# A transformer layer on one core: PE works on a constant tile before x arrives, x transposes through four banks, and the products with w_ck1 and w_cv1 go side by side

## The chip, the cores and the metric

The kernel runs on one core of a Trainium2 chip. The metric is the device time of one execution in microseconds (us). Three runs of the kernel before gave 1227.9, 1228.57 and 1229.16 us, with a median of 1228.57 us.

## The reference, cut to what matters

One layer of a decoder, everything in float32, for 256 tokens of width 1024:

```
h = rmsnorm(x, g_mix); z = h @ w_in              # 1024 -> 5184 columns
o_a = nsa_mixer(...)   # compressed, selected and windowed attention; 8 heads of 64
o_b = dsa_mixer(...)   # an indexer picks 64 keys per query; 8 heads of 64
merged = sigmoid(ga) * (o_a @ w_branch_a) + sigmoid(gb) * (o_b @ w_branch_b)
x = x + merged @ w_out
x = x + moe_ffn(rmsnorm(x, g_ffn), ...)          # top 4 of 32 experts, w_e1 1024x2048, w_e2 1024x1024
x = x + sigmoid(rmsnorm(x, g_ple) @ w_ple_gate) * (p @ w_ple)
```

Within `nsa_mixer` the compressed branch makes one key and one value from 32 tokens each, 15 of them in each of 2 groups:

```
def compress(z, pe, w1, w2):
    zb = z[:, cmp_tok] + pe[None, None, :, None, :]
    hdn = jax.nn.silu(jnp.einsum('bclgd,lde->bcge', zb, w1))    # w1: 32 x 64 x 64
    return jnp.einsum('bcge,ed->bcgd', hdn, w2)
k_cmp = rmsnorm(compress(k_cmp_raw, pe_ck, w_ck1, w_ck2), g_k)
v_cmp = compress(v_cmp_raw, pe_cv, w_cv1, w_cv2)
```

## The kernel before, in words

Each engine has its own program, written out by hand, and the engines meet in semaphores. TensorE (PE) follows the list `ORDER` at first. `T:G` transposes the gains g_mix, g_ple and g_ffn into gT. `T:X0` to `T:X3` transpose x, each two of its eight blocks of 128 columns, by four transposes of 128x128. `Z0` to `Z6` are the products with column chunks of w_in; the late chunks of w_in (the branch gates) are spread over the attention that follows. The letters `IX`, `DQ`, `DK`, `NQ`, `K`, `R` and `PE` after a `T:` are transposes of what the Z stages gave.

A job of the `T:` kind gets its PSUM bank by its place in the list `TJOBS`: `tbank(n)` returns bank 4 or 5 in turn and waits until the job two before it is evacuated (semaphore t_ev). The transposes stand at L1455. ScalarE (ACT) evacuates all of them, those of x at L891, with the gain as scale, into hT. Z0 (L1507) starts on the first pair of blocks of hT once it is evacuated, and each further pair has its own wait. Z0 has 296 columns; the chunks after it have 512. The weight chunks go through four buffers, wbuf, and SyncE (SP) issues their loads at L712: chunk 0 right behind x, chunk 1 when the second half of x has landed, and the later ones when their buffer is free.

PE's program begins with a wait on ld_const: four small loads that ACT issues at L874 to L877 (the identity, g_mix, g_ple, g_ffn). VectorE (DVE) begins with a wait for both halves of x and with the sums of squares of x (L1092), from which GpSimd (POOL) makes the root of the mean (L807, L812, semaphore x_rs). ACT needs it when it evacuates Z0 (L952). POOL's first work is a memset of the tile `half`, 128x64 times -0.5 (L795), and its chain semaphore pool_ch counts it.

The attention runs over 24 units. In step u PE issues the scores of unit u (L1554), the transposes of unit u-3 (L1562), some passes of the late chunks of w_in (L1590) and the products with the values of unit u-4 (L1577, L1581), two heads at a time with their results in partitions 0 to 63 and 64 to 127. In step 1 comes the stage `HID` (L1535), the products of the compressed branch: for keys and then for values, 16 products with a stationary tile of 128x64 and a moving tile of 128x30, both results in partitions 0 to 63 of bank 7. ACT takes its exponential (L929), DVE finishes the silu (L1269 to L1274), and in step 5 the stage `CMPKV` multiplies with w_ck2 and w_cv2 (L1541, L1543).

After the attention come the two branch products (L1623), w_out (L1644), the router, and 32 experts. The weights of an expert, 12 MB, go through a ring of ten slots of 2 MB. SP issues the first five of these loads when the last output of the attention is evacuated (o_ev, L354 in `load`), the rest when later stages of PE free the space. PE multiplies with w_e1 at L432 and with w_e2 at L461. The last stage multiplies with w_ple_gate (L1712).

In the change, `glu` of the experts counts two steps with one semaphore in place of two, so that there are semaphores for the new ones.

Of the kernel before, what the change touches and what calls it, by code (L numbers as in the profile page):

```python
# [18 lines left out]
ALU = mybir.AluOpType  # L19
# [3 lines left out]
P = 128  # L23
SEQ, DM = 256, 1024
TT = SEQ // P
# [63 lines left out]

TJOBS = [x for x in ORDER if x.startswith("T:")]  # L90
for _u in range(STEPS):
# [23 lines left out]
def block_kernel(nc, io, out):  # L115
    ctx = ExitStack()
    with ctx:
# [37 lines left out]
        def bm(ap, n):  # L155
# [55 lines left out]
        ckr = work_small(4)  # L211
        ck2w = work_small(2, DH, parts=DH)

# [60 lines left out]
            sem(n) for n in ("ld_wab", "ld_bias", "st_er", "st_rep", "ld_route", "ld_b1", "ld_be2", "ld_p", "ld_ple", "ld_ple_gate"))  # L274
        piece = [sem(f"piece{i}") for i in range(NS)]
        ld_wo = [sem(f"ld_wo{n}") for n in range(2)]
        gates_ready, zeroed, x_sq, x_rs, t_ps, t_ev, z_ps, z_ev = (
# [9 lines left out]
            sem(n) for n in ("s_ps", "s_log", "s_exp", "s_prob", "bd_ready", "o_ps", "o_ev"))  # L287
        pr_ps, pr_used, mg_ready, wo_ps, x2_ready, f_sq, f_rs = (
            sem(n) for n in ("pr_ps", "pr_used", "mg_ready", "wo_ps", "x2_ready", "f_sq", "f_rs"))
        rt_ps, lg_ready, rt_exp, m_ready, rk_ps, wr_ready, wt_ready, hp_ready, b1_sub, b1_cast, ranks_taken, x2_taken, xr_ready, dup_ready, h0_ready, oe_zero = (  # L290
# [19 lines left out]
        def expert_sems(tag):  # L310
            names = ("pieces_used", "s_ready", "sel_ready", "xe_ps", "xe_ready", "gc_ready", "lin_ready", "glu_ready", "sig_ready",
                     "act_ready", "at_ps", "at_ready", "wst_ps", "ws_ready", "wst_ready", "out_ready")
            return {n: sem(f"{n}_{tag}") for n in names}
# [306 lines left out]
        def expert_dve(ve, a):  # L620
# [20 lines left out]
            def glu(it, used):  # L641
                ve.wait_ge(s["pieces_used"], used)
                d.tensor_scalar(gc, ps[0][:, :], LIMIT, None, ALU.min).then_inc(s["gc_ready"], 1)  # L643
                d.tensor_scalar(lin, ps[1][:, :], LIMIT, -LIMIT, ALU.min, ALU.max).then_inc(s["lin_ready"], 1)
                ve.wait_ge(s["gc_ready"], it + 1)
                ve.wait_ge(s["lin_ready"], it + 1)
                d.scalar_tensor_tensor(lin, lin, 1.0, gc, ALU.add, ALU.mult).then_inc(s["glu_ready"], 1)
                ve.wait_ge(s["glu_ready"], it + 1)
                ve.wait_ge(s["sig_ready"], it + 1)
                d.tensor_tensor(act, lin, sg, ALU.mult).then_inc(s["act_ready"], 1)  # L650
# [45 lines left out]
        with nc.Block() as block:  # L696
            @block.sync
            def _(sp):
# [4 lines left out]
                for c, (o, n) in enumerate(CHUNKS):  # L703
# [9 lines left out]
                    if c == 1:  # L713
                        sp.dma_start(tab[0:BUCKETS, :], io["rel_bias"]).then_inc(ld_tab, 16)
                        sp.dma_start(tab[BUCKETS:BUCKETS + 1, :], io["negrow"]).then_inc(ld_tab, 16)
                        sp.dma_start(onehot, io["onehot"]).then_inc(ld_tab, 16)
                        sp.dma_start(const_all[:, P:545], io["consts"][:, P:545]).then_inc(ld_consts, 16)
                        for i, n in enumerate(("g_q_nsa", "g_k_nsa", "g_q_dsa", "g_k_dsa")):
                            sp.dma_start(gqk[:, i, :], io[n].to_broadcast([P, DH])).then_inc(ld_small, 16)
                        for i, n in enumerate(("pe_ck", "pe_cv")):  # L720
                            sp.dma_start(pe_in[:, i, :], io[n][0].rearrange("(l q) d -> l (q d)", q=2)).then_inc(ld_small, 16)
                        for i, n in enumerate(("w_ck2", "w_cv2")):
                            sp.dma_start(ck2w[:, i, :], io[n][0]).then_inc(ld_small, 16)
                        sp.dma_start(wr.rearrange("p (q r) n -> p q r n", r=RUN), io["w_router"][0].rearrange("(q p r) n -> p q r n", p=P, r=RUN)).then_inc(ld_route, 16)
                        sp.dma_start(br, io["b_router"].to_broadcast([P, NE])).then_inc(ld_route, 16)
# [145 lines left out]
            def _(sc):  # L871
# [6 lines left out]
                def tjob(name):  # L878
# [6 lines left out]
                    if kind == "G":  # L885
                        a.copy(gT, b[:, 0:24]).then_inc(t_ev, 1)
                        sc.wait_ge(t_ev, n + 1)
                    elif kind == "X":
                        for i in range(2):
                            k = 2 * t + i  # L890
                            l = a.activation(hTv[:, k, :], b[:, i * SEQ:(i + 1) * SEQ], ACT.Copy, scale=gT[:, k:k + 1])  # L891
                        l.then_inc(t_ev, 1)
                    elif kind == "IX":
# [30 lines left out]
                def stage_act(stage):  # L924
                    if stage.startswith("T:"):
                        tjob(stage)
                    elif stage == "HID":
                        sc.wait_ge(h_ps, 1)
                        a.activation(hsg, ps[7][0:DH, 0:60].rearrange("p (a n) -> p a n", a=2), ACT.Exp, scale=-1.0).then_inc(h_exp, 1)  # L929
# [156 lines left out]
            def _(ve):  # L1086
                d = nc.vector
                ch = Chain(ve, dve_ch)
                ve.wait_ge(ld_x, 16)
                ve.wait_ge(ld_xb, 16)  # L1090
# [137 lines left out]
                for u in range(NU + 2):  # L1228
# [37 lines left out]
                    if u == HIDDEN_AT:  # L1266
# [3 lines left out]
                        ch(d.reciprocal(hsg, hsg))  # L1270
                        ch(d.tensor_tensor(hid, hsg, ps[7][0:DH, 0:60].rearrange("p (a n) -> p a n", a=2), ALU.mult))
                        ve.wait_ge(zeroed, 1)
                        for g in range(2):
                            l = d.tensor_copy(hid4[:, g, :, 0:NCMP], bm(hid[:, 1, g * NCMP:(g + 1) * NCMP], 4))  # L1274
                        l.then_inc(hid_ready, 1)
# [157 lines left out]
            def _(te):  # L1433
                mm, tr = nc.tensor.matmul, nc.tensor.transpose
                te.wait_ge(ld_const, 16 * 4)

# [5 lines left out]
                def tjob(name):  # L1442
# [4 lines left out]
                    if kind == "G":  # L1447
                        tr(b[:, 0:16], grow, ident[0:16, 0:16])
                        for r in range(RUN):
                            l = tr(b[:, 16 + r:24:RUN], gffn[:, r:RUN * P:RUN], ident[0:KT // RUN, 0:KT // RUN])  # L1450
                    elif kind == "X":
                        te.wait_ge(ld_x if t < 2 else ld_xb, 16)
                        for i in range(2):
                            for q in range(TT):
                                l = tr(b[:, i * SEQ + q * P:i * SEQ + (q + 1) * P], x[:, q, (2 * t + i) * P:(2 * t + i + 1) * P], ident)  # L1455
                    elif kind == "IX":
# [34 lines left out]
                    l.then_inc(t_ps, 1)  # L1491

                for stage in ORDER:
                    if stage.startswith("T:"):
                        tjob(stage)
                    elif stage[0] == "Z":
# [29 lines left out]
                def stage_pe(stage):  # L1526
                    if stage.startswith("T:"):
                        tjob(stage)
                    elif stage == "HID":
                        te.wait_ge(ld_ck, 32)  # L1530
                        te.wait_ge(zb_ready, 1)
                        te.wait_ge(i_rl, 6)
                        for kv in range(2):
                            for l2 in range(16):
                                l = mm(ps[7][0:DH, kv * 30:(kv + 1) * 30], wck1[:, kv, l2, :], zb[:, kv, l2, :], start=l2 == 0, stop=l2 == 15)  # L1535
                        l.then_inc(h_ps, 1)
                    elif stage == "CMPKV":
                        te.wait_ge(hid_ready, 1)
                        te.wait_ge(o_ev, 1)
                        for g in range(2):  # L1540
                            mm(ps[6][0:NCMP, g * DH:(g + 1) * DH], hid[:, 0, g * NCMP:(g + 1) * NCMP], ck2w[:, 0, :], start=True, stop=True)  # L1541
# [224 lines left out]
```

## Time and profile before

| | |
|---|---|
| median of three runs | 1228.57 us |
| the profiled execution | 1228.02 us |
| its span, first to last instruction | 1226.1 us |
| PE busy | 1152.8 us, 94% |
| DVE, ACT, POOL busy | 271.0, 193.1, 35.8 us |
| read from HBM | 446.71 MB |
| mean over the span | 368 GB/s |

The span lies 1.9 us below the profiled execution's own time, which is 0.55 us below the median. A float32 product appears in the trace as two passes, each with a weight load (LDWEIGHTS, engine PEld) and a MATMUL (PE); a transpose has one pass. A MATMUL's duration is its latency: passes are pipelined, and the distance from start to start says what one costs.

### The profile page before, as it was taken

To read this page: it belongs to the slowest core of one execution; us is meant where nothing else is said; L and a number is where in the kernel's file an instruction comes from. 1 tells how busy PE (TensorE), PEld (TensorE's weight loads), DVE (VectorE), ACT (ScalarE), POOL (GpSimd) and SP (SyncE) were. 2 spreads that over 40 slices of the span, in tenths; PEclk is the share of its full clock that TensorE was granted. 3 is DMA by queue.
4 is the path that set the end of the run, shared out by engine and by line. 5 is a ranking of instruction groups with operands and counts; after the bars stand their busy time and mean duration, and the time that the engine had idled before them with its cause. 6 is when DMAs were issued, how large, how long until landed. Compare 5 with 4: busy or idle time off the path is not lost.

```text
span 1226.1 us, 15102 instructions
## 1 busy us (share of the span) xinstructions
PE 1152.8 (94%) x6374; PEld 490.5 (40%) x6374; DVE 271.0 (22%) x780; ACT 193.1 (16%) x411; POOL 35.8 (3%) x49
## 2 busy tenths in 40 slices
PE   7999999999999999998989889999989898988998
PEld 4455545453333343333333333333333343333344
DVE  1474543253111121111111111111112121111121
ACT  2223445131111111111111100000000010000011
POOL 2122100000000000000000000000000000000000
PEclk9999999999999999999999989999999999999999
DMA  8934070978999999999999999999999999999980
GB/s 281 333 138 172 35 206 32 416 247 346 394 432 437 429 427 431 431 435 429 431 432 435 424 430 429 433 431 430 430 433 433 432 430 433 433 431 430 425 360 35
DMA packets 39884, 448.41 MB, mean 366 GB/s; under 512 B 7407, under 2 KB 10576, under 8 KB 26306
## 3 DMA queue, kind: packets, MB, share of 16 engines
q1 hardware_dynamic: 38254, 441.66, 86.4%
q0 software_dynamic: 1264, 5.27, 1.2%
q10 hardware_dynamic: 324, 0.86, 0.3%
q8 instruction: 33, 0.54, 0.2%
q14 instruction: 9, 0.07, 0.0%
HBM read 446.71 MB, written 4.22 MB: 368 GB/s over the span
## 4 chain that ended last, share of the span: by engine, by line
PE 66%; DMA 31%; ACT 1%; issue 1%; DVE 0%; ACTq 0%
PE ps L432 21%; DMA wbuf<-in_w_e 15%; PE ps L461 12%; DMA ring<-in_w_e 12%; PE ps L1507 7%; PE ps L1590 5%; DMA wbuf<-in_w_ple_gate 3%; PE ps L404 3%; PE ps L395 3%; PE ps L1712 2%; PE ps L1623 2%; PE ps L1644 2%; PE ps L1554 2%; ACT xres L580 1%; PE ps L451 1%
## 5 line engine op out<-in xcount | busy, mean ns | idle before, releaser
L432 PE MATMUL ps<-ring,xres 128*64 128x512 f32 x1216 | 277.2, 611 | 18.1 <-DMA ring<-in_w_e 17.9
L432 PE MATMUL ps<-wbuf,xres 128*64 128x512 f32 x832 | 186.4, 602 | 11.2 <-DMA wbuf<-in_w_e 11.2
L643 DVE TENSOR_SCALAR oT<-ps 128x512 f32<-128x512 f32 x32 | 22.1, 692 | 706.1 <-PE ps L432 706.1
L432 PEld LDWEIGHTS ps<-ring,xres 128*64 128x64 f32 x1216 | 88.9, 141 | 195.2 <-issue 165.7
L461 PE MATMUL ps<-ring,xres 128*64 128x512 f32 x608 | 134.8, 595 | 12.5 <-ACT xres L580 12.5
L432 PEld LDWEIGHTS ps<-wbuf,xres 128*64 128x64 f32 x832 | 60.3, 138 | 129.7 <-issue 109.5
L461 PE MATMUL ps<-wbuf,xres 128*64 128x512 f32 x384 | 85.0, 595 | 8.1 <-ACT xres L580 8.1
L576 ACT ACTIVATE oT<-oT 128x512 f32<-128x512 f32 x30 | 18.9, 630 | 453.6 <-DVE oT L643 453.6
L1507 PE MATMUL ps<-wbuf,hT 128*128 128x512 f32 (+2 forms) x224 | 85.7, 540 | 0.0
L461 PEld LDWEIGHTS ps<-ring,xres 128*64 128x64 f32 x608 | 42.2, 137 | 91.8 <-issue 80.4
L404 PE MATMUL ps<-xres 64*128 64x512 f32 x256 | 63.6, 615 | 0.7 <-ACT xres L606 0.7
L1590 PE MATMUL ps<-wbuf,hT 128*128 128x512 f32 x128 | 59.8, 594 | 0.0
L1507 PEld LDWEIGHTS ps<-wbuf,hT 128*128 128x128 f32 x224 | 41.9, 190 | 38.8 <-issue 35.6
L395 PE MATMUL ps<-misc,gat 128*128 128x64 bf16 x1536 | 56.2, 197 | 0.5 <-DVE gat L1344 0.5
L395 PEld LDWEIGHTS ps<-misc,gat 128*128 128x128 bf16 x1536 | 56.0, 117 | 1.3 <-DVE misc L1379 1.3
L582 ACT COPY xres<-ps 128x512 f32<-128x512 f32 x30 | 17.6, 586 | 216.0 <-PE ps L461 216.0
L461 PEld LDWEIGHTS ps<-wbuf,xres 128*64 128x64 f32 x384 | 26.4, 137 | 58.4 <-issue 48.0
L404 PEld LDWEIGHTS ps<-xres 64*128 64x128 f32 x256 | 22.0, 186 | 41.8 <-issue 40.2
L618 DVE TENSOR_TENSOR xres<-ps,misc 128x512 f32<-128x512 f32 x32 | 22.1, 692 | 33.3 <-PE ps L395 33.3
L1712 PE MATMUL ps<-wbuf,ring 128*128 128x512 f32 (+1 forms) x80 | 27.9, 508 | 1.5 <-DMA wbuf<-in_w_ple_gate 1.5
L1590 PEld LDWEIGHTS ps<-wbuf,hT 128*128 128x128 f32 x128 | 22.3, 190 | 17.5 <-issue 17.4
L1644 PE MATMUL ps<-wbuf,hT 128*128 128x512 f32 x64 | 28.5, 594 | 0.0
(250 smaller groups left out, 788.7 us busy)
## 6 DMA issues: line engine op xcount, KB each, us to landing
ring<-in_w_e SPq DMA_DIRECT2D x51, 4096.0 KB, 37.2
wbuf<-in_w_e SPq DMA_DIRECT2D x36, 4096.0 KB, 37.3
ring<-in_w_e SPq DMA_DIRECT2D x14, 2048.0 KB, 28.6
wbuf<-in_w_in SPq DMA_DIRECT2D x9, 2048.0 KB, 12.5
wbuf<-in_w_e SPq DMA_DIRECT2D x4, 2048.0 KB, 11.0
wbuf<-in_w_out SPq DMA_DIRECT2D x2, 2048.0 KB, 8.5
wbuf<-in_w_ple_gate SPq DMA_DIRECT2D x2, 2048.0 KB, 41.1
rel_rows_repeated<-rel_rows POOLq DMA_DIRECT2D x1, 3072.0 KB, 17.7
```

Source lines behind the costliest of these rows:

```text
L395: l = mm(O[:, k * SLOTS:(k + 1) * SLOTS], hp[:, q, t, rows_of(k)], S[:, t, :], start=t == 0 and q == 0, stop=t == TT - 1 and q == 2)
L404: l = mm(ps[4 + 2 * t + n][:, :], wST[h, t * P:(t + 1) * P], oe[h, :], start=False, stop=False, skip_group_check=True)
L432: l = mm((G, Lb)[n // 2][(n % 2) * SLOTS:(n % 2 + 1) * SLOTS, :], xeT[:, k, :], dealt(slots[at][:, r * 2 * DFF:(r + 1) * 2 * DFF])[n], sta ...
L461: l = mm(O[n * SLOTS:(n + 1) * SLOTS, :], actT[:, r, h * SLOTS:(h + 1) * SLOTS], slots[at][:, r * DM + n * 512:r * DM + (n + 1) * 512], st ...
L618: nc.vector.tensor_tensor(xeT, ps[2][:, :].rearrange("p (k c) -> p k c", k=KT), bc(gT[:, 16:24], SLOTS), ALU.mult).then_inc(s["xe_ready"], 1)
L643: d.tensor_scalar(gc, ps[0][:, :], LIMIT, None, ALU.min).then_inc(s["gc_ready"], 1)
L1507: l = mm(ps[2 * (c % 2) + t][:, 0:n], hTv[:, k, t * P:(t + 1) * P], wv[:, k, :], start=k == 0, stop=k == KT - 1)
L1554: mm(ps[2 + u % 2][:, 0:2 * n], q[:, j, t * P:(t + 1) * P], k[:, :, 0:n], start=True, stop=True).then_inc(s_ps, 1)
L1590: l = mm(ps[t][:, :], hTv[:, k, t * P:(t + 1) * P], wbuf[:, WBUF[c] * 4096 + k * 512:WBUF[c] * 4096 + (k + 1) * 512], start=k == 0, stop=k ...
L1623: l = mm(ps[2 - 2 * (i % 2) + m_][:, :], oTv[:, m_, j, t * P:(t + 1) * P], (wa, wb)[m_][:, j, n:n + 512], start=j == 0, stop=j == 3)
L1644: l = mm(ps[(i + 2) % 4][:, :], hTv[:, k, t * P:(t + 1) * P], wo[i % 2][:, k, :], start=k == 0, stop=k == KT - 1)
L1712: l = mm(ps[4 + i % 4][:, 0:w_], x3T[:, k, t * P:(t + 1) * P], wple_g[k // 4][:, k % 4, n:n + w_], start=k == 0, stop=k == KT - 1)
```

## The change

PE runs 24 products of the constant tile `half` with itself (64 columns) into bank 7 before it waits for the constants. The transposes of x leave the list `TJOBS` and get a bank each (5, 6, 7, 4) and semaphores of their own; ACT evacuates blocks 0, 1, 4, 5 and DVE blocks 2, 3, 6, 7, ahead of its sums of squares. The products of w_ck1 and w_cv1 alternate, the second with its result in partitions 64 to 127; what follows them (hid, hsg, ck2w, hid4) is laid out accordingly.

```diff
+XBANK = [5, 6, 7, 4]
+WARM = 24
-TJOBS = [x for x in ORDER if x.startswith("T:")]
+TJOBS = [x for x in ORDER if x.startswith("T:") and not x.startswith("T:X")]
...
-        hid, hsg = work_small(2, 30, parts=DH), work_small(2, 30, parts=DH)
-        hid4 = work_small(2, 4, 32, parts=DH)
+        hid, hsg = work_small(30), work_small(30)
+        hid4 = work_small(2, 4, 32)
...
@@ ACT
+                def x_columns(t):
+                    sc.wait_ge(xt_ps, t + 1)
+                    for i in range(2):
+                        k = 2 * t + i
+                        l = a.activation(hTv[:, k, :], ps[XBANK[t]][:, i * SEQ:(i + 1) * SEQ], ACT.Copy, scale=gT[:, k:k + 1])
+                    l.then_inc(x_act, 1)
                 for stage in ORDER:
-                    if stage.startswith("T:"):
+                    if stage.startswith("T:X"):
+                        if int(stage[3:]) % 2 == 0:
+                            x_columns(int(stage[3:]))
...
@@ DVE
                 ch = Chain(ve, dve_ch)
+                ve.wait_ge(t_ev, 1)
+                for t in (1, 3):
+                    ve.wait_ge(xt_ps, t + 1)
+                    for i in range(2):
+                        k = 2 * t + i
+                        l = d.tensor_scalar(hTv[:, k, :], ps[XBANK[t]][:, i * SEQ:(i + 1) * SEQ], gT[:, k:k + 1], None, ALU.mult)
+                    l.then_inc(x_dve, 1)
                 ve.wait_ge(ld_x, 16)
...
@@ PE
+                te.wait_ge(pool_ch, 1)
+                for _ in range(WARM):
+                    mm(ps[7][0:SLOTS, 0:64], half, half, start=True, stop=True)
                 te.wait_ge(ld_const, 16 * 4)
...
+                def x_columns(t):
+                    te.wait_ge(ld_x if t < 2 else ld_xb, 16)
+                    if t == 3:
+                        te.wait_ge(t_ev, 1)
+                    for i in range(2):
+                        for q in range(TT):
+                            l = tr(ps[XBANK[t]][:, i * SEQ + q * P:i * SEQ + (q + 1) * P], x[:, q, (2 * t + i) * P:(2 * t + i + 1) * P], ident)
+                    l.then_inc(xt_ps, 1)
...
-                                    te.wait_ge(t_ev, 2 + k // 2)
+                                    te.wait_ge((x_act, x_dve)[k // 2 % 2], k // 4 + 1)
...
-                        for kv in range(2):
-                            for l2 in range(16):
-                                l = mm(ps[7][0:DH, kv * 30:(kv + 1) * 30], wck1[:, kv, l2, :], zb[:, kv, l2, :], start=l2 == 0, stop=l2 == 15)
+                        for l2 in range(16):
+                            for kv in range(2):
+                                l = mm(ps[7][kv * DH:(kv + 1) * DH, 0:30], wck1[:, kv, l2, :], zb[:, kv, l2, :], start=l2 == 0, stop=l2 == 15)
...
-                            l = mm(ps[6][:, (2 + g) * DH:(3 + g) * DH], hid4[:, g].rearrange("p j c -> p (j c)"), ck2w[:, 1, :], start=True, stop=True)
+                            l = mm(ps[6][:, (2 + g) * DH:(3 + g) * DH], hid4[DH:P, g].rearrange("p j c -> p (j c)"), ck2w[DH:P, :], start=True, stop=True)
```

## Rows read from the trace of the kernel before

**Rows 1.** The page: busy time of each engine, and the granted clock in 40 slices.

```profile
PE 1152.8 (94%) x6374; PEld 490.5 (40%) x6374; DVE 271.0 (22%) x780; ACT 193.1 (16%) x411; POOL 35.8 (3%) x49
...
PEclk9999999999999999999999989999999999999999
```

**Rows 2.** Busy time by stretch: length, engines (instructions), clock, DMA share, GB/s.

```profile
120.00:210.00 90.00, 90.00 (x422) 45.23 (x420) 40.70 (x239) 41.02 (x145) 4.70 (x5) 1.00 0.31 93
...
281.00:520.00 239.00, 232.63 (x1461) 91.87 (x1461) 41.74 (x108) 30.93 (x45) 0.00 (x0) 1.00 0.99 421
520.00:1194.00 674.00, 619.13 (x3760) 241.47 (x3756) 100.28 (x227) 63.65 (x111) 0.00 (x0) 0.97 1.00 428
```

**Rows 3.** What SP's queue waited for, 0 to 260 us: total, times, longest.

```profile
SPq L357 <- PE ps L1623: 26.2, 1, 26.2
...
SPq L354 <- ACT oT L983: 0.5, 1, 0.5
```

**Rows 4.** The chain of waits, 0 to 12 us: start, length, what.

```profile
2.17 4.55 DMA gat<-in_g_ffn
...
6.77 0.28 PE ps L1448
7.06 0.44 PE ps L1450 x4
7.50 1.06 PE ps L1455 x4
...
8.65 0.85 ACT hT L891 x2
...
9.54 1.72 PE ps L1455 x8
```

**Rows 5.** Timeline of PE, 11 to 19 us: start, time, instructions merged.

```profile
11.09 8.14 PE L1507 MATMUL ps<-wbuf,hT 128*128 128x296 f32 x32
```

**Rows 6.** Timeline of all engines, 0 to 36 us.

```profile
0.75 0.15 POOL L795 MEMSET misc<- 128x64 f32 x1 [0.29 <-POOLq L1758]
...
7.63 1.22 DVE L1092 CUSTOM_DVE_ANT_0 ring<-xres 128x1024 f32<-128x1024 f32 x1
...
9.30 0.71 POOL L812 TENSOR_TENSOR misc<-misc 128x2 f32<-128x2 f32 x1
...
15.28 0.51 ACT L952 ACTIVATE ring<-ps,misc 128x296 f32<-128x296 f32 x1 [3.02 <-PE ps L1507]
```

**Rows 7.** Loads of w_in chunks 0 and 1 (L712): issue and landing.

```profile
L712 SPq DMA_DIRECT2D wbuf<-in_w_in x1: 469/469/469, 1.8 to 1.8; - x1
...
DMA to landing us min/median/max: 8.0/8.0/8.0
...
L712 SPq DMA_DIRECT2D wbuf<-in_w_in x1: 368/368/368, 6.3 to 6.3; - x1
...
DMA to landing us min/median/max: 9.0/9.0/9.0
```

**Rows 8.** The page's groups: L643 (DVE from PSUM) and L395 (short passes).

```profile
L643 DVE TENSOR_SCALAR oT<-ps 128x512 f32<-128x512 f32 x32 | 22.1, 692 | 706.1 <-PE ps L432 706.1
...
L395 PE MATMUL ps<-misc,gat 128*128 128x64 bf16 x1536 | 56.2, 197 | 0.5 <-DVE gat L1344 0.5
```

**Rows 9.** The chain of waits, 100 to 130 us.

```profile
102.21 0.45 PE ps L1472 x4
...
110.69 3.85 PE ps L1535 x64
114.53 2.77 PE ps L1590 x6
...
128.94 0.58 PE ps L1543 x4
```

**Rows 10.** Timeline of PEld at the start of one L1535 and one L1581.

```profile
110.61 0.13 PEld L1535 LDWEIGHTS ps<-ring,wbuf 128*64 128x64 f32 x1 [0.33 <-issue]
...
210.14 0.14 PEld L1581 LDWEIGHTS ps<-ring 128*64 128x64 f32 x2 [0.76 <-issue]
```

**Rows 11.** The instructions of L1581, 210.1 to 210.7 us: duration, first and last start.

```profile
L1581 PE MATMUL ps<-ring x8: 272/273/323, 210.1 to 210.5; 128*64 128x128 f32 x8
```

More of the change, by code:

```diff
@@ L211, in block_kernel @@
         ckr = work_small(4)
-        ck2w = work_small(2, DH, parts=DH)
+        ck2w = work_small(DH)
         g0 = Take(gat)
@@ L275, in block_kernel @@
         piece = [sem(f"piece{i}") for i in range(NS)]
+        xt_ps, x_act, x_dve = (sem(n) for n in ("xt_ps", "x_act", "x_dve"))
         ld_wo = [sem(f"ld_wo{n}") for n in range(2)]
@@ L287, in block_kernel @@
             sem(n) for n in ("s_ps", "s_log", "s_exp", "s_prob", "bd_ready", "o_ps", "o_ev"))
-        pr_ps, pr_used, mg_ready, wo_ps, x2_ready, f_sq, f_rs = (
-            sem(n) for n in ("pr_ps", "pr_used", "mg_ready", "wo_ps", "x2_ready", "f_sq", "f_rs"))
+        pr_ps, pr_used, wo_ps, x2_ready, f_sq, f_rs = (
+            sem(n) for n in ("pr_ps", "pr_used", "wo_ps", "x2_ready", "f_sq", "f_rs"))
         rt_ps, lg_ready, rt_exp, m_ready, rk_ps, wr_ready, wt_ready, hp_ready, b1_sub, b1_cast, ranks_taken, x2_taken, xr_ready, dup_ready, h0_ready, oe_zero = (
@@ L887, in tjob @@
                         sc.wait_ge(t_ev, n + 1)
[L888 to L892, printed above, removed]
                     elif kind == "IX":
@@ L928, in stage_act @@
                         sc.wait_ge(h_ps, 1)
-                        a.activation(hsg, ps[7][0:DH, 0:60].rearrange("p (a n) -> p a n", a=2), ACT.Exp, scale=-1.0).then_inc(h_exp, 1)
+                        a.activation(hsg, ps[7][:, 0:30], ACT.Exp, scale=-1.0).then_inc(h_exp, 1)
                     elif stage == "CMPKV":
@@ L936, in stage_act @@
                         l.then_inc(v4_ready, 1)
+                def x_columns(t):
[4 more added lines that the diff above has]
+                    l.then_inc(x_act, 1)
                 for stage in ORDER:
-                    if stage.startswith("T:"):
+                    if stage.startswith("T:X"):
+                        if int(stage[3:]) % 2 == 0:
+                            x_columns(int(stage[3:]))
+                    elif stage.startswith("T:"):
                         tjob(stage)
@@ L1270, in _ @@
                         ch(d.reciprocal(hsg, hsg))
[L1271 removed]
+                        ch(d.tensor_tensor(hid, hsg, ps[7][:, 0:30], ALU.mult))
                         ve.wait_ge(zeroed, 1)
                         for g in range(2):
[L1274 removed]
+                            l = d.tensor_copy(hid4[DH:P, g, :, 0:NCMP], bm(hid[DH:P, g * NCMP:(g + 1) * NCMP], 4))
                         l.then_inc(hid_ready, 1)
@@ L1450, in tjob @@
                             l = tr(b[:, 16 + r:24:RUN], gffn[:, r:RUN * P:RUN], ident[0:KT // RUN, 0:KT // RUN])
[L1451 to L1455, printed above, removed]
                     elif kind == "IX":
@@ L1491, in tjob @@
                     l.then_inc(t_ps, 1)
+                def x_columns(t):
[6 more added lines that the diff above has]
+                    l.then_inc(xt_ps, 1)
                 for stage in ORDER:
-                    if stage.startswith("T:"):
+                    if stage.startswith("T:X"):
+                        x_columns(int(stage[3:]))
+                    elif stage.startswith("T:"):
                         tjob(stage)
@@ L1540, in stage_pe @@
                         for g in range(2):
-                            mm(ps[6][0:NCMP, g * DH:(g + 1) * DH], hid[:, 0, g * NCMP:(g + 1) * NCMP], ck2w[:, 0, :], start=True, stop=True)
+                            mm(ps[6][0:NCMP, g * DH:(g + 1) * DH], hid[0:DH, g * NCMP:(g + 1) * NCMP], ck2w[0:DH, :], start=True, stop=True)
                         for g in range(2):
-                            l = mm(ps[6][:, (2 + g) * DH:(3 + g) * DH], hid4[:, g].rearrange("p j c -> p (j c)"), ck2w[:, 1, :], start=True, stop=True)
+                            l = mm(ps[6][:, (2 + g) * DH:(3 + g) * DH], hid4[DH:P, g].rearrange("p j c -> p (j c)"), ck2w[DH:P, :], start=True, stop=True)
                         l.then_inc(kc_ps, 1)
```

12 lines of the change are left out of this document (6 added, 6 removed).

## The prediction

> **What bounds the kernel now.** I read the page first: PE is busy 94% of the span, no other engine over a quarter [rows 1]. That is an average, so I cut the span into stretches. From 120 to 210 us PE has no idle time at all (90.00 of 90.00 us) and the DMA engines are a third busy; from 281 us on the DMA engines are at 0.99 and 1.00 with 421 to 428 GB/s, up to 1194 us [rows 2]. The kernel thus has two parts: up to the end of the attention the end is set by PE, and behind it by the stream of expert weights. The change lies wholly in the first part, so the question is whether a gain there moves the stream. SP's waits answer it: the first five loads of the stream wait for the last output of the attention, and went out 0.5 us after SP was ready for them; the next wait for the branch products on PE [rows 3]. A full stream that starts x us earlier ends x us earlier. So I count what PE saves before 211 us, and take it over whole.
>
> The clock row of the page says nine tenths or more in all slices but one [rows 1], yet durations show the lower of PE's two levels at the beginning. Eight transpose passes from 9.54 us took 1.72 us, 215 ns each for 128 columns [rows 4]; four later ones of the same size took 0.45 us, 112 ns each [rows 9]. That is 1.2 against 2.4 GHz. Z0's 32 passes of 296 columns took 8.14 us, 254 ns each or 0.86 ns a column, from 11.09 us on: already at 2.4 GHz [rows 5]. So the clock rose around 11 us, about 4.2 us after PE's first instruction at 6.77.
>
> **Part 1, the head: constant tile, four banks, two engines.** Before, the order is: last constant landed at 2.17 + 4.55 = 6.72 us; gains transposed 6.77 to 7.43; eight transposes of x; a halt for ACT, which frees the bank at 9.49 (PE stood for 0.35 us: last pass begun 8.98, its slot over at 9.19, next at 9.54); eight more; Z0's first pass at 11.09 [rows 4, 5].
>
> The constant tile: 24 products are 48 passes of 64 columns. At the lower level a column costs 215/128 = 1.68 ns, so a pass 107 ns and all 5.2 us. They start when POOL's memset is through, 0.75 + 0.15 = 0.90 us [rows 6], say at 1.0, and end by 6.2 us. The constants land at 6.72, so the new work is hidden by that wait, with 0.5 us to spare. Before, the clock was up 4.2 us after PE began; counted from 1.0 us this gives 5.2 us, well before the first transpose of x.
>
> The transposes: gains at 6.77 as before, x from 7.43, 16 passes at 112 ns = 1.8 us, no bank wait, done at 9.2. Now something else is late. Chunk 0 of w_in was issued at 1.8 us and landed 8.0 us later, at 9.8 [rows 7]. So Z0 starts at 9.8 and not at 9.2; 0.6 us of the possible gain stays in this load. Even if the clock rose only at 8.5 us (five passes at 215, eleven at 112 ns: 2.3 us) the load would come last. Gain: 11.09 - 9.8 = 1.3 us. Bounds: with a clock that rises no earlier than before, 16 passes at 215 ns end at 10.87, gain 0.2 us; if chunk 0 landed before the transposes end, 1.9 us. I take 1.3.
>
> Evacuation: DVE's tile op from PSUM took 692 ns for 512 columns [rows 8], so I put 256 columns at 0.35 to 0.5 us each. Blocks 0 and 1 are ready about 0.85 us after ACT gets them (L891 x2 [rows 4]), at 8.9; DVE has 2 and 3 by 9.5, and Z0 asks for them at 9.8 + 1.0. All hidden by the load of chunk 0.
>
> What queues behind DVE's new waits: its sums of squares (L1092). They ended at 8.85, POOL's root at 10.01; ACT used it at 15.28 [rows 6]. Now DVE has blocks 6 and 7 out at 10.1 to 10.4, two sums at 1.2 us bring it to 12.8, and POOL's 1.2 us to 14.0. ACT can want it at 9.8 + 16 passes of 0.254 = 13.9 plus 0.2. It is a tie. If it is late by a few tenths, only ACT's evacuation of Z0 waits, and PE needs these two banks again only for Z2, behind the 14 us of Z1. Cost: nothing.
>
> Z1 needs chunk 1, issued at 6.3 and landed 9.0 later, at 15.3 [rows 7]; Z1 comes after 9.8 + 8.1 = 17.9. Covered by 2.6 us. The later chunks are asked for when PE frees buffers, and moved with it.
>
> **Part 2, HID.** Its 64 passes took 3.85 us, 60 ns each [rows 9], while 30 columns at 0.86 ns stream in 26 ns. So the pass is bound by its weight load, and the loads follow one another: 30 ns into the first only one has begun. In L1581, where two heads write partitions 0 to 63 and 64 to 127, two loads of the same shape have begun within 30 ns [rows 10], and its eight passes of 128 columns start within some 0.4 us, where one after the other they need 7 x 112 = 0.8 [rows 11]. Both loads and streams of the two halves overlap. Alternating kv gives HID just this form. 32 pairs at 60 ns would be 1.9 us. The other limit is the rate at which passes can be handed over: L395's 1536 passes were busy 56.2 us, 37 ns each [rows 8]; two of them in 74 ns would make 2.4 us. The shape is that of L1581, so I take the lower value with a small surcharge, 2.05 us; gain 1.8. Bounds: no overlap, 0; streams alone, 32 x 26 = 0.8 us, gain 3.0. What is late next in the attention? PE itself: it has no idle time from 120 to 210 us [rows 2], and DVE and ACT are below half busy there, so the gain stays.
>
> The Trainium skill ("TensorE: Matmul & The Clock Gate", Part 3, The mechanism) says that a weight load overlaps running matmuls only where the row group differs. By that rule HID would keep its 3.85 us, since its halves differ in columns. Rows 10 speak against it here.
>
> CMPKV: its value half moves to rows 64 to 127; L1543 x4 took 0.58 us [rows 9]. Between 0 and 0.2 us of gain, taken as 0. DVE's silu works on 30 columns rather than 60, off the path. The merged semaphore of the experts changes no wait: 0.
>
> **Sum.** 1.3 + 1.8 = 3.1 us. The profiled execution would go from 1228.02 us (span 1226.1, and 1.9 around it) to 1224.9. The median of the runs is 0.55 us above it; from there 1228.57 - 3.1 = 1225.5 us.
>
> **The rivals.**
>
> A. Both parts work: 1225.5 us, in its own range 1224.4 to 1226.4 (HID from 2.4 down to 1.7 us, some tenths of spread between runs).
>
> B. HID doesn't overlap. The head alone remains: 1228.57 - 1.3 = 1227.3. For it: LDWEIGHTS bounds HID, and in L1581 the streams, not the loads, fill the time. Against: rows 10. The page's rule named above gives this case.
>
> C. The constant tile does not raise the clock in time, as its 64 columns fill only half of the array. The transposes run at 215 ns: 1228.57 - 0.2 - 1.8 = 1226.6. Against: sparse and short passes stood at the start before, and the clock still rose in 4.2 us [rows 4].
>
> D. The stream swallows the gain: the load rate near 281 us and not the release of the slots decides when the stream is full. Then 0 to 0.5 us remain: 1228.3. Against: the first loads went out within 0.5 us of their release, and later ones are gated by PE [rows 3].
>
> E. Slower. Stationary and moving operand, and the place of the result, are the same in all 48 passes; if each had to wait for the last one to finish, it would cost its latency, 0.28 us as the first pass of PE at the low clock took [rows 4]. 48 x 0.28 = 13.4 us, up to 14.4; gains 0.66 and transposes 1.8, Z0 at 16.9, 5.8 us later than before, less 1.8 of HID: 1232.6. It turns to a loss when a pass costs over 0.2 us. Against: passes into the same bank in HID stood 60 ns apart at latencies over 200.
>
> **How the numbers follow.** A 0.68, B 0.08, C 0.10, D 0.09, E 0.05. About 0.2% (2.5 us) is what a measurement of this kernel can tell from no change, so faster means below 1226.1 us. A lies on that side in about nine of ten cases, as its lower gains (HID at 2.4 us, an early load wait) come near the bound: 0.62. B, C, D and the rest of A are within: 0.32. E and unknown losses: 0.06. The range from 1224.2 to 1227.7 us holds A, B and C; D and E stay outside.
>
> **What would show it.** Right: PE's 48 short passes end before 6.7 us; transposes of x 110 ns apart; Z0's first pass at 9.8 us, held by the load of chunk 0; HID in about 2.0 us with pairs of loads a few ns apart; every stage after it 3.1 us earlier, SP's first expert load and the last one too. Wrong: transposes 215 ns apart (C), HID at 3.8 us (B), the constant tile still running at 7 us (E), or a gain at 211 us that is smaller at the end (D).

## The result, and the profile after

The kernel with the change takes 1230.68 us (median of 16 runs, 1229.54 to 1234.06), the one before 1228.53 us in the same session (16 runs, 1227.41 to 1230.36). The ratio is 1.0019, 95% interval 1.0012 to 1.0026: 2.15 us slower, where I had forecast 3.1 us faster. The profiled execution took 1229.87 us with a span of 1227.7, against 1228.02 and 1226.1.

First the page of the kernel after, answering to [rows 1]; its last line is a row of the DMA queues (packets, MB, share of 16 engines' span), which I had not read ahead of the prediction.

```profile
PE 1152.8 (94%) x6422; PEld 492.7 (40%) x6422; DVE 272.1 (22%) x784; ACT 191.4 (16%) x407; POOL 35.7 (3%) x49
...
PEclk9999999999999999999999999999999999999999
...
q8 instruction: 61, 1.00, 0.3%
```

The same row in the page before:

```profile
q8 instruction: 33, 0.54, 0.2%
```

PE's busy time is the same to 0.1 us, with 48 passes more. What differs is the number of 16 KB packets with instructions (queue q8, kind "instruction"): 61 for 33.

**The head.** The timeline of PE after, 0 to 20 us [rows 4, 5]:

```profile
0.95 5.38 PE L1453 MATMUL ps<-misc 128*64 128x64 f32 x48 [0.95 <-POOL misc L798]
7.61 0.23 PE L1467 MATMUL ps<-misc,gat 16*128 16x16 f32 x1 [1.27 <-DMA gat<-in_g_ffn]
...
8.24 1.96 PE L1514 MATMUL ps<-misc,xres 128*128 128x128 f32 x16
10.16 8.24 PE L1533 MATMUL ps<-wbuf,hT 128*128 128x296 f32 x32
```

The constant tile ends at 6.33 us, the sixteen transposes stand 110 ns apart (1.96 less one latency, by 15), and Z0 starts at 10.16. The constants landed 0.8 us later than before, at 7.56 (gains at 7.61, not 6.77); why is open. PE reached the gains at 7.60 to 7.84 us in three of the five profiles with a constant tile (this one, 5 and 6 below), and at 6.70 to 6.81 in all five without. Chunk 0 of w_in took 8.3 us from its issue at 1.8 [rows 7], so it landed at 10.1:

```profile
L715 SPq DMA_DIRECT2D wbuf<-in_w_in x1: 469/469/469, 1.8 to 1.8; - x1
...
DMA to landing us min/median/max: 8.3/8.3/8.3
```

ACT's first evacuation of Z0 now waits for POOL's root (timeline of ACT [rows 6]), the tie that I had named; it starts 0.6 us earlier than before, and no matmul waited for it.

```profile
14.64 0.51 ACT L961 ACTIVATE ring<-ps,misc 128x296 f32<-128x296 f32 x1 [4.00 <-POOL misc L815]
```

**HID and the end of the attention.** The chain after, at HID [rows 9], and at the last output of the attention:

```profile
109.85 1.99 PE ps L1561 x64
...
208.15 0.27 ACT oT L992
...
208.56 3.67 PE ps L1649 x8
```

HID fell from 3.85 to 1.99 us: its weight loads now start in pairs, 7 ns apart, with 55 to 58 ns from pair to pair, where before each started 55 to 59 ns behind the last. SP's waits for these stages [rows 3] kept their lengths:

```profile
SPq L360 <- PE ps L1649: 26.2, 1, 26.2
...
SPq L357 <- ACT oT L992: 0.5, 1, 0.5
```

SP issued the first expert load at 208.44 us, before at 211.13: 2.69 us earlier. Up to here the prediction held, at 2.7 for 3.1 us.

**The stream.** The stretches after, columns as in [rows 2]:

```profile
120.00:210.00 90.00, 89.54 (x425) 44.90 (x425) 38.65 (x231) 41.69 (x144) 3.63 (x5) 1.00 0.31 91
281.00:520.00 239.00, 232.84 (x1464) 91.77 (x1462) 39.63 (x94) 32.77 (x47) 0.00 (x0) 1.00 0.99 422
520.00:1194.00 674.00, 614.53 (x3738) 240.88 (x3734) 99.85 (x227) 61.62 (x109) 0.00 (x0) 0.98 1.00 426
270.90:273.40 2.50, 2.50 (x12) 1.12 (x11) 2.32 (x9) 1.22 (x3) 0.41 (x1) 1.00 0.98 419
```

The DMA share is 1.00 from 520 to 1194 us in both, but 426 instead of 428 GB/s moved. Each GB/s less is 0.67 MB over these 674 us, or 1.6 us of the stream; as both are rounded, 1.6 to 4.7 us.

The last row is the stage before the experts. At the same place the kernel before shows this stretch:

```profile
273.60:277.20 3.60, 3.60 (x10) 1.34 (x10) 2.17 (x8) 2.31 (x4) 0.00 (x0) 0.53 0.96 410
```

Here the granted clock was 0.53 (passes 0.86 us apart, not 0.43: 1.2 against 2.4 GHz), and 1.00 after. This gave the profile after another 1.6 us, so that the first expert started 4.27 us earlier. It doesn't hang on the change: of the ten profiles of this document one more has the clock low there, that of experiment 5, which has the change, and those of 1, 3, 7 and 8 do not. How often the kernel before has it in its other runs is not known.

Now the landings. The weights come in loads of 4 MB; undisturbed, one lands each 9.71 us. I followed all landings of both kernels in order and list those whose step was longer by more than 0.6 us, from 315 us on (the step at 696 us, 13.0 us in both, is left out: two other loads lie in it):

```
before: landing, extra step | after: landing, extra step | after against before, behind it
321.19  +1.20               | 318.22  +3.72              | -3.0
332.13  +1.24               |                            | -4.2
498.76  +1.26               | 484.85  +1.48              | -4.2
                            | 602.96  +1.47              | -2.8
                            | 743.84  +1.53              | -1.3
795.02  +1.30               |                            | -2.6
                            | 861.92  +1.52              | -1.2
                            | 999.47  +1.52              | +0.35
                            | 1161.31 +1.51 (2 MB load)  | +1.87
```

A lead of 4.2 us was kept for some 260 us (landings at 328 to 592 us after), and then lost in steps of 1.5 us, between which next to nothing changes. At 484.85 and 498.76 us both kernels have such a step, at different loads. One step in rows: loads of the kernel after, with issue (last numbers of the first line) and time to landing:

```profile
L367 SPq DMA_DIRECT2D ring<-in_w_e x1: 328/328/328, 946.8 to 946.8; - x1
...
DMA to landing us min/median/max: 41.4/41.4/41.4
...
L367 SPq DMA_DIRECT2D wbuf<-in_w_e x1: 327/327/327, 959.1 to 959.1; - x1
...
DMA to landing us min/median/max: 40.4/40.4/40.4
```

and of the kernel before:

```profile
L364 SPq DMA_DIRECT2D ring<-in_w_e x1: 328/328/328, 948.0 to 948.0; - x1
...
DMA to landing us min/median/max: 41.4/41.4/41.4
...
L364 SPq DMA_DIRECT2D wbuf<-in_w_e x1: 327/327/327, 960.2 to 960.2; - x1
...
DMA to landing us min/median/max: 38.9/38.9/38.9
```

Before, the second lands at 999.1, 9.7 us behind the first (989.4). After, both are issued 1.2 us earlier, but the second lands 11.3 us behind the first (988.2, 999.5): 0.4 us later than before.

What stands at these places is queue q8. Its packets by stretch: 538 to 703 us, the second round of PE's first loop over experts, before:

```profile
q1 hardware_dynamic: 2938, 71.14, 100.4%
```

and after, then 840 to 1132 us, its second loop, after and before:

```profile
q1 hardware_dynamic: 2932, 70.68, 100.0%
q8 instruction: 10, 0.16, 0.4%
```

```profile
q1 hardware_dynamic: 4307, 125.47, 100.0%
q8 instruction: 16, 0.26, 0.4%
```

```profile
q1 hardware_dynamic: 4327, 126.06, 100.3%
```

Before, PE fetches no instructions in these stretches; after, it does so all the time. The q8 packets that come just ahead of the late landings after are numbers 19, 27, 35, 43, 51 and 59 of the trace: every eighth. Number 11 comes just ahead of 318.22. Before they are number 11 ahead of 332.13, 19 ahead of 498.76 and 27 ahead of 795.02, so the kernel before pays for such packets too, only for fewer of them. The landing at 321.19 before has no packet ahead of it; by its place it may belong to the filling of the stream.

PE's program shows it too. The timeline after, around the head of that round:

```profile
536.46 6.61 PE L464 MATMUL ps<-ring,xres 128*64 128x512 f32 x30
544.89 0.64 PE L423 MATMUL ps<-gat,misc 96*64 96x512 bf16 x4 [1.83 <-issue]
545.37 4.88 PE L435 MATMUL ps<-ring,xres 128*64 128x512 f32 x21
550.78 1.50 PE L435 MATMUL ps<-ring,xres 128*64 128x512 f32 x6 [0.52 <-issue]
```

and before:

```profile
540.16 7.09 PE L461 MATMUL ps<-ring,xres 128*64 128x512 f32 x32 [0.68 <-ACT xres L580]
547.08 0.62 PE L420 MATMUL ps<-gat,misc 96*64 96x512 bf16 x4
547.53 7.04 PE L432 MATMUL ps<-ring,xres 128*64 128x512 f32 x32
```

PE stood still for 1.83 and 0.52 us where it waited for no engine and no load.

**Theory.** PE's program has two loops over experts (five visits a round; round 0 stands ahead of them, rounds 1 and 2 are the first, 3 to 5 the second), so the first can be fetched again once and the second twice. One round is 1650 instructions. A packet of 16 KB holds some 256: between packet 1 and packet 21 of the kernel before (33.62 to 532.04 us) PE started 2502 weight loads and 2502 MATMULs, 250 a packet, and waits and branches come on top. So an instruction has 64 bytes and a round 105.6 KB. The change puts 93 instructions more ahead of both loops. Where a loop starts within a 16 KB piece then decides whether its body stays in PE's instruction memory or is fetched again in every round, and every eighth fetch holds the full stream up by 1 to 1.5 us. **Rivals:** the side-by-side HID, the reordered DVE or the earlier issue of loads upsets the stream; the executed passes of the constant tile cost something by themselves; it is PE's halts, and not the fetches, that delay the loads.

The Trainium skill ("Runtime: NRT & Kernel Launch", Instruction fetch mechanics) describes such a memory of 2048 instructions, filled in blocks of 256. The 16 KB packets and the count above agree with it. It also says that a taken branch whose target isn't in the current window of two pages forces a fetch; the kernel before doesn't bear that out, as PE goes back over 1650 instructions at some 547 us and no packet comes between 532.04 and 706.57 us. It calls the crossing of a block's boundary mostly hidden; behind a full weight stream it is not, as the runs below show. By its size alone such a memory would hold any of these bodies, so why some are fetched again no run here explains.

### The profile page after: what moved, and what is told of

Read it like the earlier page. It is cut to its first block, busy times and chain, and to the rows that moved or that the text cites. A ratio compares the mean times of both kernels' runs of the same rounds, so it can differ in the third digit from the quotient of the medians.

```text
span 1227.7 us, 15227 instructions
## 1 busy us (share of the span) xinstructions
PE 1152.8 (94%) x6422; PEld 492.7 (40%) x6422; DVE 272.1 (22%) x784; ACT 191.4 (16%) x407; POOL 35.7 (3%) x49
## 4 chain that ended last, share of the span: by engine, by line
PE 65%; DMA 32%; ACT 1%; issue 1%; DVE 0%; ACTq 0%
PE ps L435 20%; DMA wbuf<-in_w_e 19%; PE ps L464 12%; DMA ring<-in_w_e 9%; PE ps L1533 7%; PE ps L1616 5%; DMA wbuf<-in_w_ple_gate 4%; PE ps L407 3%; PE ps L398 3%; PE ps L1738 2%; PE ps L1649 2%; PE ps L1670 2%; PE ps L1580 2%; ACT xres L583 1%; PE ps L454 1%
## 5 line engine op out<-in xcount | busy, mean ns | idle before, releaser
L1616 PE MATMUL ps<-wbuf,hT 128*128 128x512 f32 x128 | 59.8, 594 | 0.0
L423 PE MATMUL ps<-gat,misc 96*64 96x512 bf16 x128 | 20.5, 399 | 14.2 <-issue 13.9
## 6 DMA issues: line engine op xcount, KB each, us to landing
wbuf<-in_w_e SPq DMA_DIRECT2D x4, 2048.0 KB, 11.3
```

Source lines behind the costliest of these rows:

```text
L1616: l = mm(ps[t][:, :], hTv[:, k, t * P:(t + 1) * P], wbuf[:, WBUF[c] * 4096 + k * 512:WBUF[c] * 4096 + (k + 1) * 512], start=k == 0, stop=k ...
```

## The experiments

All ratios are against the kernel before, measured beside each on the same chip; its median was 1227.9 us in both sessions. The kernel with the change was not run again in them, so what is set against it compares two ratios. Experiment 8 is a single run.

**1. The kernel before, with products that are never executed.** A jump over 23 products ahead of PE's first wait: 95 instructions in the program, of which only a register move and a branch run.

```diff
+                never = te.alloc_register("never")
+                te.reg_mov(never, 0)
+                with te.If_ne(never, 0):
+                    for _ in range(23):
+                        mm(ps[7][0:SLOTS, 0:64], half, half, start=True, stop=True)
                 te.wait_ge(ld_const, 16 * 4)
```

> The kernel before, with 95 instructions put into PE's program before its first wait: a jump over 23 products that are never executed. Nothing else changes, nothing more is executed than a register move and a branch. Theory F (code position): the body of each expert loop, 1650 instructions of 64 bytes, ends in one more 16 KB piece of code, so PE fetches it anew in every iteration; instruction packets of queue q8 rise from 33 to about 60, and each eighth of them costs the weight stream 1.5 us: 4 x 1.5 = 6 us, 1234.5 us. Theory H (the stream swallows a gain, or the constant tile or the earlier start harms it): code that isn't executed changes nothing, 1228.5 us and 33 packets.

Measured: 1233.91 us (5 runs, 1233.18 to 1234.85), ratio 1.005 [1.0036, 1.0063]: 6.0 us slower. From its page:

```profile
q8 instruction: 61, 1.00, 0.3%
```

Its second round of the first loop has the 10 packets and the halt of the kernel after; the timeline of PE:

```profile
539.92 7.09 PE L461 MATMUL ps<-ring,xres 128*64 128x512 f32 x32 [0.68 <-ACT xres L580]
548.88 0.64 PE L420 MATMUL ps<-gat,misc 96*64 96x512 bf16 x4 [1.87 <-issue]
549.35 4.88 PE L432 MATMUL ps<-ring,xres 128*64 128x512 f32 x21
554.45 1.93 PE L432 MATMUL ps<-ring,xres 128*64 128x512 f32 x8 [0.21 <-issue]
```

Its landings are late at 488.3, 606.4, 747.3, 865.4, 1002.9 and 1169.7 us, by 1.0 to 1.07 each; the first five are the same loads as after. That is 6.2 us where after has 9.0 at its six; the rest is lost here in steps of 0.1 to 0.4 us, each at a landing right behind one of the packets between the eighths, and the sum over the stream is the same (below). So nothing of HID, the transposes or the executed tile is needed for the loss.

**2. The change, with 131 instructions more** (the same jump over 32 products, behind the constant tile; again only a register move and a branch run). It moves the loops on to the next piece.

> The kernel after, with 131 instructions more before the loops, of which only a register move and a branch are executed; with the 93 of the change the loops are then 224 instructions behind their place in the kernel before, nearly a whole piece of 256. Theory F: the loop bodies fit again, q8 shows about 33 packets, and the gain of the head and of HID (2.7 us at 211 us in the trace) arrives at the end: 1225.8 us, or less by the time of a slow stretch of PE's clock at 274 us. Theory H: as after, 1230.7 us.

Measured: 1224.79 us (11 runs, 1224.48 to 1226.67), ratio 0.9976 [0.9967, 0.9985]. The page is back at

```profile
q8 instruction: 33, 0.54, 0.2%
```

and no step of its landings from 281 us on is over 0.6 us longer than the same one before. The change as a whole, executed in full and in a longer program, is 3.1 us faster than the kernel before, and 5.3 us faster than the change as it was made (0.0043 between the two ratios). Experiment 1 makes the loss with nothing of the change, and this one takes it away with all of it: the place of the loops is the cause.

**3. HID alone,** in the kernel before; no instruction is added (hid, hsg, ck2w and hid4 laid out as in the change).

```diff
-                        for kv in range(2):
-                            for l2 in range(16):
-                                l = mm(ps[7][0:DH, kv * 30:(kv + 1) * 30], wck1[:, kv, l2, :], zb[:, kv, l2, :], start=l2 == 0, stop=l2 == 15)
+                        for l2 in range(16):
+                            for kv in range(2):
+                                l = mm(ps[7][kv * DH:(kv + 1) * DH, 0:30], wck1[:, kv, l2, :], zb[:, kv, l2, :], start=l2 == 0, stop=l2 == 15)
```

> The kernel before with the products of w_ck1 and w_cv1 side by side and nothing else of the change; PE's program has as many instructions as before. Theory F: no more fetches (33 packets), HID in 2.0 instead of 3.85 us, and the gain reaches the end: 1226.7 us. Theory H: a gain before the weight stream is swallowed by it: 1228.5 us.

Measured: 1226.56 us (11 runs, 1224.78 to 1228.78), ratio 0.9986 [0.9977, 0.9995], 34 packets on q8. 1.3 to 1.7 us are gained at the end, and the chain shows the 1.99 us of the kernel after:

```profile
111.98 1.99 PE ps L1535 x64
```

**4. The change without the constant tile.**

```diff
-                te.wait_ge(pool_ch, 1)
-                for _ in range(WARM):
-                    mm(ps[7][0:SLOTS, 0:64], half, half, start=True, stop=True)
                 te.wait_ge(ld_const, 16 * 4)
```

> The kernel after without the constant tile: four banks, evacuation by two engines and HID side by side; PE's program is 3 instructions shorter than before. Theory F: 33 packets; x transposes at 1.2 GHz as before, so the head gains only 0.2 to 0.5 us, HID 1.9: 1226.3 us. Theory H with the constant tile as the culprit gives the same; with the earlier start as the culprit 1228.5 us or more.

Measured: 1225.6 us (11 runs, 1224.7 to 1227.42), ratio 0.9981 [0.9972, 0.999], 32 packets. The part that was to bring the clock up cost the change 4.7 us (1.0019 - 0.9981 of 1228).

**5. The change with a wide tile:** three products of 512 columns, the same 3072 columns of passes in 12 instructions for 96.

```diff
-                for _ in range(WARM):
-                    mm(ps[7][0:SLOTS, 0:64], half, half, start=True, stop=True)
+                for _ in range(3):
+                    mm(ps[7][0:SLOTS, :], half, bm(half, 8), start=True, stop=True)
```

> The kernel after with the same 5.1 us of constant work written as 3 products of 512 columns (the tile half repeated by a zero stride) in place of 24 of 64: 12 instructions and not 96, so the expert loops stand 9 behind their place in the kernel before. Theory F (the loops' place in the code): 32 to 34 packets on q8, transposes of x 110 ns apart, all of the gain at the end: 1224.9 us beside 1227.9 of the kernel before. Rival C2 (the constant tile itself costs the stream, by power or clock): as after, 1230.7 us.

Measured: 1224.47 us (8 runs, 1223.27 to 1227.86), ratio 0.9977 [0.9967, 0.9987], 34 packets. It keeps PE as busy as the tile of the change, as its timeline shows, and loses nothing. Its median is the lowest of all, but 2 and 4 are not told from it, and three of its eight runs took 1227.1 to 1227.9 us, the profiled one among them. The transposes came out at 110 ns only in part, since the clock fell at 9.9 us:

```profile
0.95 5.38 PE L1453 MATMUL ps<-misc 128*64 128x512 f32 x6 [0.95 <-POOL misc L798]
...
8.47 2.40 PE L1514 MATMUL ps<-misc,xres 128*128 128x128 f32 x16
```

**6. The change with `WARM = 16`,** 32 instructions fewer.

> The kernel after with 16 constant products and not 24: the loops stand 61 instructions behind their place in the kernel before. The second loop stands 45 nearer to its piece's start than the first. Theory F with a bound between the two: the first loop is fetched anew in its second iteration, the second loop not; about 42 packets on q8, one or two delays of 1.5 us instead of four: 1226.5 us. If neither crosses: 33 packets and 1224.9 us; if both: 61 and 1230.7 us.

Measured: 1226.52 us (11 runs, 1225.78 to 1229.11), ratio 0.9992 [0.9983, 1.0001]. From its page:

```profile
q8 instruction: 43, 0.70, 0.2%
```

Ten packets fall into 538 to 703 us, none into 840 to 1132: the first loop is fetched again, the second is not. It is 2.0 us slower than experiment 5; the two intervals overlap, so the times alone don't settle this one, but the trace has one late landing of 1.4 us more than the kernel before (486.2, 604.3 and 745.2 us behind its packets 19, 27 and 35).

**7. The kernel before with 23 products between the two loops,** in a branch that is never taken. Only the second loop moves.

```diff
                 with te.If(n_max > SLOTS):
                     scatter_of(PLE_AFTER - 1).then_inc(flushed, 1)
+                    for _ in range(23):
+                        mm(ps[3][0:SLOTS, 0:64], half, half, start=True, stop=True)
                     expert_pe(te, rest)
```

> The kernel before with 23 products (92 instructions) in the branch that runs only when an expert has over 64 tokens, which never happens here; it stands between the two expert loops, so the second loop moves by 92 and the first stays. Theory F: up to 703 us as before, then about 19 fetches more in the three iterations of the second loop, 52 packets in all, two or three delays of 1.5 us: 1227.9 + 3.5 = 1231.4 us. If PE's halts at the loop's head and not the fetches cost the time, the same total, but the landings of weights fall back at the halts and not at each eighth fetch.

Measured: 1230.62 us (7 runs, 1229.91 to 1232.51), ratio 1.0023 [1.0012, 1.0034]: 2.7 us slower. Its queues in 840 to 1132 us (538 to 703 has no q8 packet):

```profile
q1 hardware_dynamic: 4302, 125.27, 99.9%
q8 instruction: 18, 0.29, 0.4%
```

The late landings fall behind packets and not at PE's halts, as the theory has it, but not in the form expected (two or three of 1.5 us): they come closer together and are smaller, seven of 0.73 to 0.95 us between 715 and 1079 us.

**8. The wide tile alone, in the kernel before.**

```diff
+                te.wait_ge(pool_ch, 1)
+                for _ in range(3):
+                    mm(ps[7][0:SLOTS, :], half, bm(half, 8), start=True, stop=True)
                 te.wait_ge(ld_const, 16 * 4)
```

> The kernel before with 3 wide constant products at PE's start (12 instructions) and nothing else of the change. Theory: the transposes of x run 110 ns apart, but the two banks and ACT alone as evacuator hold them up: X2 waits for the evacuation of X0, X3 for that of X1, so Z0 starts at about 10.5 us and not 11.1; 33 packets on q8. If Z0 starts at 11.1 all the same, two banks set the head and not the clock.

Measured: one run of 1226.86 us, span 1224.8. The first eight transposes ran at the upper level, and then, behind the halt for the bank, the clock had fallen (eight in 1.87 us); Z0 began at 10.62:

```profile
7.31 1.09 PE L1458 MATMUL ps<-misc,xres 128*128 128x128 f32 x8
8.96 1.87 PE L1458 MATMUL ps<-misc,xres 128*128 128x128 f32 x8 [0.56 <-ACT hT L891]
```

**All together.** I counted the instructions ahead of each loop in PE's program, modulo 256 (one packet):

```
kernel        loop 1   loop 2   fetched again   q8 packets   against before
before          49        4     no,  no             33         -
3 HID only      49        4     no,  no             34         0.9986
4 no tile       46        1     no,  no             32         0.9981
5 wide tile     58       13     no,  no             34         0.9977
8 tile only     61       16     no,  no             34         (one run)
2 skip, after   17      228     no,  no             33         0.9976
7 pad loop 2    49       96     no,  yes            52         1.0023
6 WARM = 16    110       65     yes, no             43         0.9992
after          142       97     yes, yes            61         1.0019
1 skip, before 144       99     yes, yes            61         1.005
```

Starts at 228 and from 1 to 65 stay resident, starts from 96 to 144 do not. 1650 instructions are six pieces and 114 more, so a body touches seven pieces from 143 of the 256 starts and eight from the others. The border in the table fits seven against eight, if my count begins 47 to 77 instructions late; this is argued, not shown. The loss goes with the packets: 28 more cost 6.0 us (1 against before) and 5.3 us (after against 2), 19 more 2.7 us, 9 more 2.0 us (6 against 5, within the noise).

The traces say it without the head and the clock. From the landing of the fifteenth expert load (332.13 us in the kernel before) to that of the last one (1183.92) pass 851.8 us before and 851.7 to 851.9 in 2, 4, 5 and 8, with 20 or 21 packets between; 853.3 us in 6 with 31, 855.5 in 7 with 39, and 857.9 both after and in 1, with 49. Only 3 doesn't fit: 853.3 us with 21 packets, in a profiled run that was the slowest of its eleven (1228.78 us). So the number of packets doesn't account for every late landing.

## Why the prediction was wrong, step by step

**"A full stream that starts x us earlier ends x us earlier": failed.** It held for some 260 us, and over the stretches where PE's loops are not fetched again, and it holds at the end where the loops keep their place (experiments 2 to 5). In the change itself it did not, since the rate of the stream was not the same. From 332 us on six landings are late, 9.0 us in all, instead of two with 2.6: 6.5 us lost, less some 0.4 that the kernel before loses in steps of a tenth. With the lead of 4.2 us this gives 1.9 later, and the last load landed 1.67 us later (1195.78 against 1194.11).

**The constant tile, "hidden by that wait": right on the path that I looked at, wrong as the whole cost.** Its execution is covered, with 1.2 us to spare. I had priced 96 instructions by their duration and not by their place in the program. By it they move both loops to starts from which they are fetched again, 28 packets more, and cost what experiment 4 gives back, 4.7 us. This step failed; none of my rivals had it, and E, the one on this side, was a latency that didn't occur (passes 110 ns apart or closer).

**Head, 1.3 us: mis-sized.** This profile has 0.93 (11.09 to 10.16), since constants and chunk 0 landed later. In the other profiles with the tile Z0 began at 10.91 (2), 10.66 (5), 11.44 (6) and 10.62 (8), without it at 11.09 to 11.31 in four kernels and at 10.93 with four banks alone (4). The four with the whole change (after, 2, 5, 6) start Z0 at 10.79 on average, 0.4 us before the four without; at Z1's first pass, which takes in the clock under Z0, it is 20.09 against 20.60 us. In the kernel after, the tile ran at the lower level (5.38 us for 48 passes, 112 ns each) and the transposes at the upper. In experiment 2 its passes took 95 ns on average, so the clock rose before its end; PE then waited 1.29 us for the constants, and the sixteen transposes took 3.33 us, 208 ns each. In experiment 6 they were as slow. Rival C thus came true in two of four profiles, once by a way that it didn't name: the clock had risen and fell back behind the wait. The granted clock reads 0.5 from 7.9 us on in experiment 2, from 8.5 in 6, from 9.1 in 8 and from 9.9 in 5, up to 11.3 to 13.3 us, so in 5 Z0's first passes too ran at the lower level; of the five profiles with a tile only the one after has no such stretch. In experiment 2 the clock didn't even decide: chunk 0 of w_in took 9.09 us and landed at 10.87, 0.04 us ahead of Z0, where it landed between 9.59 and 10.12 in the nine others. The timeline of PE in experiment 2:

```profile
0.96 4.58 PE L1453 MATMUL ps<-misc 128*64 128x64 f32 x48 [0.96 <-POOL misc L798]
...
7.46 3.33 PE L1519 MATMUL ps<-misc,xres 128*128 128x128 f32 x16
```

Whether the tile is worth anything at all is open: experiments 2 and 5 with it are 0.8 and 1.1 us below 4 without it, within their intervals.

**HID, 2.05 us: right.** 1.99 measured, in two profiles, and experiment 3 gives it back in the runs. Rival B fell with it.

**Evacuation, DVE's waits, the merged semaphore, CMPKV: right,** cost nothing that shows. The tie at POOL's root came, and was harmless.

**Rival D** (the stream swallows the gain) fell as I had put it: the lead was there at 281 us and for long after. Without the fetches a gain at 211 us comes out at the end, as experiments 2 and 4 show. That experiment 2 measures 3.1 us, just what I had forecast, is partly luck: in its profile SP's first expert load went out 1.77 us earlier than before, in that of experiment 4 1.88, and the 3.6 and 3.5 us at the last landing hold another 1.6 from the stretch of low clock at 274 us, which my sum doesn't have. Whether the medians hold it too is not known.

**Rival of the halts:** PE's 1.83 us at the head of the round did not move one landing at that place (552.92 and 562.63, both still 4.23 us early), as loads for some 40 us ahead were queued. What is late are single landings, mostly at an eighth fetch. Open is why: the packets themselves are small. 28 of them are 0.46 MB, which at 428 GB/s is 1.1 us and not 6, each takes mostly 1.0 to 1.1 us, and which of the DMA engines they share with the weights was not shown.

## What to carry to other kernels

Count an added instruction twice: as execution, and as length ahead of every loop behind it. Compare the packets of the instruction queue in both profiles first, when a change that only adds cheap instructions ends up slower than its parts; padding that never runs, or the same work in fewer and wider instructions, tells and mends it. A gain that reaches a saturated stream is kept only if the stream's rate stays, so follow its landings one by one and not only its start and its share.

## What the runs showed of the hardware

- A loop of 1650 PE instructions (105.6 KB) is kept or fetched again in every round, 9 to 10 packets of 16 KB a round, by its start in a piece of 256 instructions. This is worth 6.0 us of 1228 (experiment 1), with nothing more executed than a register move and a branch.
- Under a weight stream at 428 GB/s where a load of 4 MB lands each 9.71 us, the landing behind each eighth fetch is late by 1.0 to 1.6 us in eight of the ten profiles. The seven between move a landing by at most some 0.15 us after and by up to 0.43 in experiment 1; in 7 the delays came twice as often and half as large, and 3 is irregular.
- PE stood still for 1.83 us (after) and 1.87 us (1) at the head of a round that was fetched again.
- Weight loads and streams of passes into partitions 0 to 63 and 64 to 127 overlap: 64 passes of 30 columns in 1.99 us for 3.85.
- PE's clock behind the constant tile differs from profile to profile of the same instructions: up during the tile and down again behind a wait of 1.29 us in experiment 2 (transposes 208 ns apart), low during the tile and up behind a wait of 1.27 us in the profile after (110 ns apart).
